# A decoder step's second norm: the eight sample rows applied by POOL, their store placed ahead of the last tile's

## What is computed

```
def layer_norm(x, g, b, eps=1e-5):
    mu = x.mean(-1, keepdims=True)
    var = square(x - mu).mean(-1, keepdims=True)
    return (x - mu) * rsqrt(var + eps) * g + b
...
f = moe(x)
x = layer_norm(ALPHA * x + f, ln2_g, ln2_b)      # y_prompt (512 x 1024), y_sample (8 x 1024)
```

## Time and profile before

| what | value |
|---|---|
| time, median of 3 runs | 1152.08 us (1149.71 to 1156.97) |
| time of the profiled execution | 1150.96 us |
| span of the profiled execution | 1148.6 us |
| busy: PE, DVE, ACT, POOL | 1081.4, 537.3, 280.1, 180.3 us |

### The profile page before, as it was taken

How to read it: one execution, slowest core, us unless ns; L and a number is a source line. 1 busy time by engine, 2 the same in 40 slices (tenths; PEclk the granted TensorE clock), 3 DMA queues, 4 the chain that set the end, 5 groups by cost and what they waited for, 6 DMA issues and landing times.

```text
span 1148.6 us, 33461 instructions
## 1 busy us (share of the span) xinstructions
PE 1081.4 (94%) x14966; PEld 820.4 (71%) x14967; DVE 537.3 (47%) x1204; ACT 280.1 (24%) x596; POOL 180.3 (16%) x198
## 2 busy tenths in 40 slices
PE   8999998888989999999999999999999999999990
PEld 6877886766653467777777777777777777777760
DVE  0888959699565787553222222222222222222215
ACT  2156411132427111111111111111111111111114
POOL 2000100000000002122222222222222122222310
PEclk9999998988679999999999999999999999999996
DMA  7222231320416547799999999999999999999724
GB/s 214 74 56 56 55 82 35 55 68 5 161 39 225 183 162 296 287 358 367 368 363 366 372 359 359 362 361 358 368 369 353 355 368 359 360 360 360 217 37 159
DMA packets 87364, 278.79 MB, mean 243 GB/s; under 512 B 22331, under 2 KB 46916, under 8 KB 62381
## 3 DMA queue, kind: packets, MB, share of 16 engines
q1 hardware_dynamic: 71941, 239.29, 56.9%
q0 software_dynamic: 14336, 34.11, 12.4%
q10 hardware_dynamic: 944, 3.24, 0.8%
HBM read 258.80 MB, written 34.52 MB: 255 GB/s over the span
## 4 chain that ended last, share of the span: by engine, by line
PE 67%; DVE 9%; ACT 2%; issue 2%; DMA 1%; SPq 0%; POOLq 0%; DVEq 0%; ACTq 0%
PE ph L2297 30%; PE ph L2325 19%; PE pst L2272 4%; PE ph L1498 2%; PE pz_late L2272 2%; DVE w_exp L163 2%; PE ph L1453 1%; PE pt L869 1%; PE pst L1392 1%; PE ph L1624 1%; PE ph L1480 1%; PE pz_late L1436 1%; PE pz_late L1437 1%; PE pt L1411 0%; PE pz_late L1521 0%
## 5 line engine op out<-in xcount | busy, mean ns | idle before, releaser
L2297 PE MATMUL ph<-arena,w_exp 128*64 128x96 f32 x8192 | 352.6, 247 | 0.0
L2297 PEld LDWEIGHTS ph<-arena,w_exp 128*64 128x64 f32 x8192 | 340.5, 138 | 4.2 <-issue 3.1
L2325 PE MATMUL ph<-w_exp,arena 128*96 128x512 f32 x512 | 230.5, 593 | 1.5 <-DVE arena L2315 1.5
L2352 POOL DMA_INDIRECT scr_f<-arena,row x64 | 91.9, 1436 | 472.2 <-DVE row L889 265.2
L2313 DVE TENSOR_TENSOR arena<-arena,ph 128x192 f32<-128x192 f32 x64 | 22.7, 354 | 294.3 <-ACT arena L2306 294.3
L507 PE MATMUL pz<-w_exp 128*128 128x260 f32 x672 | 158.8, 394 | 0.3 <-ACT w_exp L322 0.3
L2325 PEld LDWEIGHTS ph<-w_exp,arena 128*96 128x96 f32 x512 | 80.2, 167 | 104.0 <-issue 102.3
L507 PEld LDWEIGHTS pz<-w_exp 128*128 128x128 f32 x672 | 129.6, 196 | 23.7 <-issue 3.1
L2343 DVE TENSOR_SCALAR arena<-ph,weight 96x512 f32<-96x512 f32 x64 | 47.8, 746 | 168.0 <-PE ph L2325 167.9
L2306 ACT ACTIVATE arena<-ph 128x192 f32<-128x192 f32 x64 | 21.1, 330 | 426.1 <-PE ph L2297 419.4
L163 DVE SCALAR_TENSOR_TENSOR w_exp<-arena,w_exp 128x512 f32<-128x512 f32 x120 | 90.0, 750 | 3.8
(11 more groups left out here) (358 smaller groups left out, 1083.5 us busy)
## 6 DMA issues: line engine op xcount, KB each, us to landing
w_exp<-in_exp_up_dram SPq DMA_DIRECT2D x64, 1024.0 KB
w_exp<-in_exp_down_dram SPq DMA_DIRECT2D x64, 1024.0 KB
w_exp<-in_exp_gate_dram SPq DMA_DIRECT2D x64, 1024.0 KB
w_exp<-in_w_in_dram SPq DMA_DIRECT2D x22, 512.0 KB, 3.9
w_exp<-in_x_prompt_dram SPq DMA_DIRECT2D x8, 512.0 KB, 5.3
w_exp<-in_w_out_dram SPq DMA_DIRECT2D x2, 2048.0 KB, 11.5
scr_x<-arena SPq DMA_DIRECT2D x4, 512.0 KB
scr_f<-arena ACTq DMA_DIRECT2D x4, 512.0 KB, 4.5
```

The lines of the kernel that those rows point to most:

```text
L2297: last = nc.tensor.matmul(pgu[64 * half:64 * half + 64, s % 2, (2 * part + j) * CAP:(2 * part + j + 1) * CAP], w[job.slot][:, k, f0:P * ha ...
L2325: last = nc.tensor.matmul(pyl[0:CAP, c, :], hid[:, s % 2, j, :], m.expert_down[job.slot][:, j, c * 512:(c + 1) * 512], start=(j == 0), sto ...
L2352: nc.gpsimd.indirect_dma_start(m.scr_f, bass.IndirectOffsetOnAxis(ap=row[:, job.l:job.l + 1], axis=0), y_list[:, s % 2, :], None, bounds_c ...
```

## The change

DVE keeps the sample rows' statistics and their reciprocal, and loses their scale and shift. POOL gets three instructions after its last one: (x - mean) * reciprocal, times g, plus b, each waiting for the one before. DVE's waits on `scaled` are renumbered. SP still loads in the old order, but stores the tiles in the order 0, 1, 2, sample, 3; the sample's store waits for POOL's third instruction.

```diff
@@ sync
-        for at, i in enumerate(ORDER):
+        for i in range(NT):
             t0, n = TOK_TILES[i]
-            sp.wait_ge(out_ready, at + 1)
-            dst = m.y_prompt[t0:t0 + n, :] if i < TM else m.y_sample
-            sp.dma_start(dst, f_scaled[i][0:n, :]).then_inc(out_stored, 16)
+            if i < TM - 1:
+                sp.wait_ge(out_ready, i + 1)
+                sp.dma_start(m.y_prompt[t0:t0 + n, :], f_scaled[i][0:n, :]).then_inc(out_stored, 16)
+            elif i == TM - 1:
+                sp.wait_ge(sample_out, 3)
+                sp.dma_start(m.y_sample, f_scaled[TM][0:B, :]).then_inc(out_stored, 16)
+            else:
+                sp.wait_ge(out_ready, TM)
+                sp.dma_start(m.y_prompt[t0 - P:t0, :], f_scaled[TM - 1][0:P, :]).then_inc(out_stored, 16)
         sp.wait_ge(out_stored, 16 * NT)
@@ shift_row
-        dve.wait_ge(scaled, at + 1)
+        dve.wait_ge(scaled, i + 1)
@@ vector
         dve.wait_ge(stats_ready, 2)
-        scale_row(dve, i)
         invert_root(dve, 0, i)
-        shift_row(dve, 0, i)
         for i in range(TM):
@@ gpsimd
         pool.sem_inc(overflow_over)
+
+        i = NT - 1
+        x, out = f[i][0:B, :], f_scaled[i][0:B, :]
+        pool.wait_ge(ln2_loaded, 32)
+        pool.wait_ge(f_loaded[i], 16)
+        pool.wait_ge(inverted, 1)
+        nc.gpsimd.tensor_scalar(out, x, aggr[0:B, i, 0:1], aggr[0:B, i, 3:4], ALU.subtract, ALU.mult).then_inc(sample_out, 1)
+        pool.wait_ge(sample_out, 1)
+        nc.gpsimd.tensor_tensor(out, out, ln2_g[0:B, :], ALU.mult).then_inc(sample_out, 1)
+        pool.wait_ge(sample_out, 2)
+        nc.gpsimd.tensor_tensor(out, out, ln2_b[0:B, :], ALU.add).then_inc(sample_out, 1)
```

More of the change, by code:

```diff
@@ L2221, in experts @@
     inverted = sem("ln2_inverted")
+    sample_out = sem("ln2_sample_out")
     scaled = sem("ln2_scaled")
```

## The result

The changed kernel takes 1159.68 us in the median of 20 runs (1157.21 to 1163.06), the kernel before 1154.45 in 20 runs (1149.71 to 1158.08). The ratio is 1.0042, 95% interval 1.0031 to 1.0053: 0.42% slower, 3.6 to 6.1 us, where 0.33% had been forecast. The median of before is 2.4 us above that of its first three runs, which is most of why 1155.8 us was named and 1159.7 came.

A forecast was written before the change was run, and what follows sets the result against it. DVE was taken to bound the last stage, then the last store. Turns with POOL (+3.67 us) and the store (+0.08) gave +3.75, so 1154.7 by the profiled run and 1155.8 us at the median; range 1150.5 to 1159.5.

The forecast's parts named there:

- DVE loses two instructions and wins 0.41 us: Last stage: of 2.54 us removed from DVE only 0.41 are left, because scale 1 needs ACT's mean 1.
- POOL and DVE take turns: Last stage: POOL's instructions and DVE's scales and shifts block each other; last shift ends 3.67 us later; chance 0.72.
- The rule: DVE instruction with two SBUF inputs against POOL reading SBUF: the second stands still until the first has ended.
- Which instructions are hit: Last stage: shift 0 and scale 2 recorded with 3 us and more instead of 1.28.
- the tensor_scalar's 1.1 us: POOL's first instruction on the sample rows: taken as 1.1 us, near the memset's 0.95; upper case 2.34.
- The stores: End of the span: last store goes without waiting for POOL; the sample's 32 KB ahead of it cost 0.08 us.
- The total: Whole kernel: +3.67 for the turns and +0.08 for the store make +3.75 us.
- No collision: Rival, last stage: eight partitions don't block DVE, or not for long; 1151.7 us, chance 0.13.
- POOL starves: Rival: DVE keeps its turn, POOL finishes after it and the sample's store holds the last tile's; 1156.7 us, chance 0.10.
- POOL is slow: Rival: POOL's instructions take several times longer, DVE stands still and the store waits; over 1% from +11.5 us; chance 0.04.
- The full offload: Rival: the whole 2.5 us taken off DVE is won; 1149.6 us, chance 0.01.
- the first rival: The no-collision rival: eight partitions don't block DVE, or not for long; 1151.7 us, chance 0.13.

The follow-up runs named there:

- PSUM kernels: Changed kernel with DVE reading g and b from PSUM: ratio 1.0009 to the kernel before; with the sample's store also issued by ACT: 0.9996.
- The PSUM kernel: Changed kernel with g and b copied by ACT into PSUM and read there by DVE's scales and shifts: ratio 1.0009 to the kernel before.
- the half columns: Changed kernel with POOL's two tensor_tensor over 512 of the 1024 columns: ratio 1.0011 to the kernel before.
- the tensor_scalar alone: Changed kernel without POOL's two tensor_tensor, so the sample rows get neither g nor b: ratio 1.0005 to the kernel before.

## Why the prediction was right

- *DVE loses two instructions and wins 0.41 us.* Right. Wherever nothing is stretched (PSUM kernels), the last shift ends at 11.32 to 11.33 us instead of 11.81, 0.48 less; scale 1 waits for mean 1, 0.77 us in the profile after.
- *POOL and DVE take turns.* Right for POOL's tensor_tensor, in mechanism and price: the second one stands, then 2.20 and 1.09 us (2.2 and 1.14 forecast); 3.61 us in sum, 3.67 forecast. The PSUM kernel, the half columns and the tensor_scalar alone show cause and size. The rule was too wide: that the second stands until the first has ended does not hold for POOL's tensor_scalar, which kept DVE out for 1.0 of its 3.7 us.
- *Which instructions are hit.* Wrong: shift 0 and scale 2 were named, shift 1 and scale 3 were it. The step that failed is the tensor_scalar's 1.1 us, which was put "near the memset"; it takes 3.79 alone, more than the upper bound of 2.34 too. The sum came out all the same, since it keeps DVE out for only 1.0 us of its length, and the two encounters with tensor_tensor fell on a busy DVE whichever they were. That is luck in part, two errors that cancel: by the forecast's own rule, with DVE held for the whole length, the price would have been some 2.7 us more (3.79 less 1.1).
- *The stores.* The last tile's store did not wait for POOL, as forecast, but the sample's 32 KB ahead of it cost 0.6 us, not 0.08: the term was sized by the full rate of 406 GB/s. Where tile 2's store was over 3 us ahead, 0.1 us was measured, near that figure.
- *The total*: +3.75 forecast, +4.30 in the profiles, +3.6 to +6.1 by the timed runs. The median of before moved up by 2.4 us with more runs. By that the measured 1159.68 us stands 0.2 above the upper end of the range, 1159.5, though the ratio to before, 1.0042, is well below the 1.0064 that this end makes with the 1152.08 it was worked out from.
- *The rivals.* No collision: refuted by the two rows of 3.18 and 3.35 us. POOL starves: refuted, it got every second turn. POOL is slow: its tensor_scalar was, without reaching the store. (The 4 us more for each of the three, said there to be needed for 1%, is too high by the forecast's own sum: 11.5 - 3.75 = 7.75, or 2.6 for each.) The full offload: the ceiling is 0.4 us.
- *A reading that was off*: 94% of the span is PE's busy share and not the expert loop. The loop's matmuls (L2297) run from 475 to 1117 us, some 56%. Nothing in the sum used it.
- *Missed*: POOL's closing drain. In the changed kernel it was hidden by 0.6 us and cost nothing; had the collision been absent, as in the first rival, it would have ended the span at about 15.8 us behind the reciprocal, as it did in the two PSUM kernels, where the kernel before has 14.8; the first rival's 1151.7 could not have come out either.

## What to carry to other kernels

Before work is moved to an engine because that engine idles, look for rows in which the two run side by side, and read both durations: DVE's instructions with two inputs in SBUF and POOL's tensor_tensor exclude each other here, and one operand in PSUM frees both. Then ask what the removed work was in front of: 2.54 us of DVE bought 0.4, because ACT's mean was next. And the last few us of a program have rules of their own: a small store between the last two large ones, or a late instruction on POOL that nobody waits for, each lengthened the span.

## What had not been expected of the hardware

- POOL's last compute instruction is followed by 6.6 us of drain before the program can end (6.53 to 6.63 in the nine kernels in which it computes in the last stage); the profile names that wait after PE's sequencer. Where the program's first block ends, POOL's drain is over 0.1 us behind its copy (in the profile of the kernel before: a drain of 744 ns from 189.3 on, beside a copy that ends at 189.92). What makes the difference is open.
- POOL's tensor_scalar with two operations and two columns of scalars takes 3.79 us over 8 x 1024, its tensor_tensor 2.35; yet the first keeps DVE's two-input instructions out for 1.0 us only, the second for all of its time.
- Eight rows of 4 KB stored right behind one store of 512 KB and ahead of the next delay the landing of the second by 0.6 us; eight rows of 256 bytes don't, and with the first store over 3 us earlier it is 0.1.
